# A two-network transformer trunk in fp32: first norm on its own loads, memory tokens normalized once, the keys' side of HGRN on GpSimd, rotary tables made during a network's first product

## The chip, the cores and the metric

The kernel runs on one core of a Trainium2 chip. A core has TensorE (PE, matrix products into PSUM banks), VectorE (DVE), ScalarE (ACT), GpSimd (POOL) and SyncE (SP, here only an issuer of DMAs). The metric is the device time of one execution, in microseconds (us). The kernel before has a median of 3372.84 us over 3 runs (3372.38 to 3385.61).

## The reference

The input is 256 tokens of width 1024, everything in float32. First come two layers of three mixers side by side, all fed by one norm and one wide projection; then a second trunk of two layers with SwiGLU networks, memory attention, and a convolution or a latent attention (MLA) as mixer.

```python
for l in range(2):                                   # the first trunk
    h = rmsnorm(x, norm_g[l]); proj = h @ w_in[l]    # width 1024 -> 19,712
    y_a = hgrn2_mixer(a_q, a_ff, a_fb, a_i, lbs[l])  # both directions, summed
    y_b = retention_mixer(b_q, b_k, b_v)             # rotary, both directions
    y_c = rwkv7_mixer(c_s)                           # delta rule, both directions
    x = x + (g0*(y_a @ w_a) + g1*(y_b @ w_b) + g2*(y_c @ w_c)) @ w_out[l]
x = rmsnorm(x, final_norm_g)
...
# second trunk, layer 0: network f00, convolution + memory, network f01
#               layer 1: shared keys and values from x, network f10, MLA queries + memory, network f11
def memory_attention(q_mem, mem, mem_norm_g, w_mem_kv, g_q, g_k):
    k, v = jnp.split(rms_norm(mem, mem_norm_g) @ w_mem_kv, 2, axis=-1)   # the same mem in both layers
    ...
def chunk_gla(q, k, v, log_f, strict):   # HGRN: o_t = q_t S_t, S_t = diag(f_t) S_(t-1) + k_t^T v_t
    decay = exp(b_i - b_j)               # b: cumulative sum of log f, per channel
    scores = sum(q_i * k_j * decay, axis=-1)
```

## The kernel before, in words

Each engine runs a program of its own, written in Python generators; semaphores (`then_inc`, `wait_ge`) tie them together. Weights come in chunks of up to 1 MB through a ring of five slots that SyncE fills in the order of use (`load_chunk`, L387). Every product is fp32; each matmul that the program writes is shown as two in the trace.

In the first trunk a layer's three mixers are woven together: R is RWKV, H is HGRN, B is retention. `weave` (L371) takes steps of three generators in the order of a string of the table `ORDER` (L144), one string for each engine; "R5 H2" means five steps of R and then two of H. So the order of the instructions on an engine is fixed by hand, and an engine that waits holds up all that stands behind it. Each mixer works in four quarters of two heads (RWKV: four) each.

**HGRN's levels** (`hgrn_dve` L1393, `hgrn_act` L1333, `hgrn_pe` L1280). The scores of a quarter are built in eight levels of block size, 128, 64, 32, ... 1. For each level VectorE makes the logarithms of the queries' and of the keys' decay (tiles `hg_qs` and `hg_ks`; L1454 to L1459 or L1474 to L1478), ScalarE takes Exp of both (L1373, L1374), VectorE multiplies them with the queries (L1481, 128x512) and the two halves of the keys (L1484, L1485, 128x256 each), TensorE multiplies keys and queries (L1311), and VectorE copies the block into the scores under a mask (L1494). Each level reuses the two tiles, so level n+1 begins when level n's product is done. GpSimd does only memsets and a few DMAs (`rwkv_pool`, L1015).

**A norm** (`norm_act` L456, `norm_dve` L478, `norm_pe` L440): per half of the tokens ScalarE sums squares (L463), VectorE makes the mean (L484), ScalarE the root (L467), VectorE the reciprocal (L487) and a diagonal matrix (L489), with which TensorE transposes and scales x (L450). VectorE and ScalarE copy the result with the gain to `h_features` (L497, L473). At the program's start VectorE and ScalarE wait for all three tables of constants (vectors, float constants, masks; L2945 to L2947) and make the lower bounds of HGRN before the first norm.

**The second trunk.** A SwiGLU network (`ffn_pe` L1836, `ffn_dve` L1994, `ffn_act` L1911) has 22 first products, one per weight chunk, with sums of operands made by VectorE two chunks ahead (`ffn_sums_dve`), and then 11 second products. Ahead of the convolution mixer and ahead of the queries the memory tokens are normalized: ScalarE squares them (L2213), takes the root (L2217), VectorE scales them into `mem_normed` (L2247). It is done once in each layer; since the tile `mem_tokens` is loaded twice (L2933, L2940), `mem_normed` also serves the networks as working space. Ahead of the shared keys VectorE makes the angles for the rotary tables (`rope_dve`, L2431, 17 small instructions with waits between) and ScalarE their Sines (`rope_act`, L2467).

## Time and profile before

| | us |
|---|---|
| median of 3 runs (lowest to highest) | 3372.84 (3372.38 to 3385.61) |
| the profiled execution's own time | 3378.15 |
| its span in the trace | 3376.3 |
| TensorE busy | 3126.1 (93%) |
| VectorE busy | 1762.8 (52%) |
| ScalarE busy | 709.1 (21%) |
| GpSimd busy | 61.5 (2%) |

The first trunk takes the first 2150 us or so (its first mixer layer 27 to 1082, its second up to 2147), the four networks 203 us each, and the rest are the mixers of the second trunk. Busy shares are means over these stages. A row of the timeline has its start, its length, the engine, the line of the kernel, what is written and read, and in square brackets how long the engine was idle before it and what released it.

### The profile page before, as it was taken

The numbers are of one execution on the slowest core, as the hardware profiler recorded it, in microseconds if no ns is written. First come the engines' busy times: TensorE is split into PE (matmuls) and PEld (weight loads), VectorE is DVE, ScalarE is ACT, GpSimd is POOL, SyncE is SP. The second block draws the span as 40 slices with busy tenths as digits, with TensorE's granted clock in tenths as the row PEclk, the third lists the DMA queues.
The fourth block names the chain that finished last, engine by engine and source line by source line (L and its number), as shares of the span: only waits on it lengthen the run. The fifth ranks groups of instructions, "written<-read, shape, count | busy, mean of one in ns | idle before, by whom it ended". The sixth has DMA issues, their size and how long they took to land.

```text
span 3376.3 us, 42896 instructions
## 1 busy us (share of the span) xinstructions
PE 3126.1 (93%) x17716; PEld 2610.1 (77%) x17716; DVE 1762.8 (52%) x3799; ACT 709.1 (21%) x1383; POOL 61.5 (2%) x70
## 2 busy tenths in 40 slices
PE   7999998999989999999899999899989979998999
PEld 6888887888876878788788887695849749855694
DVE  3555756374321474655646332475237647646475
ACT  2233323232111231332323110100111011013100
POOL 0000000000000000000000000000000000000000
PEclk9999998999989999999899999999989989997999
DMA  4323232324323422321331433444425423431343
GB/s 191 107 96 116 76 117 85 118 83 140 107 99 137 140 83 85 127 93 63 128 108 48 158 118 115 145 171 160 155 77 175 167 102 131 172 115 75 118 170 125
DMA packets 154018, 404.79 MB, mean 120 GB/s; under 512 B 57536, under 2 KB 106816, under 8 KB 109920
## 3 DMA queue, kind: packets, MB, share of 16 engines
q1 hardware_dynamic: 51376, 367.87, 30.4%
q10 hardware_dynamic: 100608, 28.32, 3.5%
q0 software_dynamic: 1840, 5.84, 0.5%
q8 instruction: 142, 2.33, 0.3%
q14 instruction: 52, 0.43, 0.0%
HBM read 389.41 MB, written 12.59 MB: 119 GB/s over the span
## 4 chain that ended last, share of the span: by engine, by line
PE 82%; DVE 10%; DMA 6%; issue 1%; ACT 1%; ACTq 0%; SPq 0%; DVEq 0%
PE bank L412 24%; PE bank L1865 16%; PE bank L1883 6%; PE bank L429 6%; PE bank L1689 5%; PE bank L1752 3%; PE bank L804 2%; DMA xT_scratch<-rw_bm 2%; PE bank L823 2%; PE bank L1311 2%; DMA rw_sig<-scores_scratch 1%; PE bank L1894 1%; DMA rw_ex<-xT_scratch 1%; DVE rw_ex L641 1%; PE bank L814 1%
## 5 line engine op out<-in xcount | busy, mean ns | idle before, releaser
L412 PE MATMUL bank<-h_features,weight_ring 128*128 128x256 f32 x4256 | 966.1, 383 | 7.4 <-DMA weight_ring<-in_w_in 2.9
L412 PEld LDWEIGHTS bank<-h_features,weight_ring 128*128 128x128 f32 x4256 | 802.1, 191 | 120.6 <-issue 5.7
L429 PE MATMUL bank<-weight_ring,h_features 128*128 128x256 f32 (+2 forms) x896 | 201.4, 376 | 2.6 <-DVE h_features L497 2.0
L429 PEld LDWEIGHTS bank<-weight_ring,h_features 128*128 128x128 f32 x896 | 161.5, 190 | 26.9 <-issue 4.0
L1865 PE MATMUL bank<-h_features,weight_ring 128*128 128x128 f32 x1408 | 171.9, 275 | 5.4 <-DVE h_features L497 5.4
L1865 PEld LDWEIGHTS bank<-h_features,weight_ring 128*128 128x128 f32 x1408 | 164.3, 192 | 6.1 <-DVE h_features L497 6.1
L1929 ACT COPY mem_normed<-bank 128x128 f32<-128x128 f32 x88 | 23.5, 267 | 485.9 <-PE bank L1865 474.6
L1689 PE MATMUL bank<-y_features,weight_ring 128*128 128x256 f32 x512 | 121.1, 384 | 0.0
L2006 DVE TENSOR_TENSOR mem_normed<-mem_normed,bank 128x256 f32<-128x256 f32 x88 | 37.1, 421 | 135.8 <-PE bank L1865 135.8
L1689 PEld LDWEIGHTS bank<-y_features,weight_ring 128*128 128x128 f32 x512 | 95.4, 191 | 12.8 <-issue 0.7
L450 PE MATMUL bank<-norm_diag,x_tokens 128*128 128x128 f32 x288 | 45.6, 330 | 58.8 <-DVE norm_diag L489 58.7
L804 PE MATMUL bank<-rw_bm,rw_scored_a 128*128 128x64 f32 x512 | 71.2, 285 | 27.1 <-DMA rw_ex<-xT_scratch 27.1
L1311 PE MATMUL bank<-hg_qs,hg_ks 128*128 128x128 f32 x512 | 76.0, 294 | 20.1 <-DVE hg_ks L1485 20.1
L450 PEld LDWEIGHTS bank<-norm_diag,x_tokens 128*128 128x128 f32 x288 | 43.6, 242 | 65.2 <-DVE norm_diag L489 44.9
L1865 PE MATMUL bank<-h_features,y_hgrn_features 128*128 128x128 f32 x704 | 93.0, 275 | 0.0
L1865 PE MATMUL bank<-y_rwkv_features,y_features 128*128 128x128 f32 x704 | 93.0, 275 | 0.0
L1865 PE MATMUL bank<-h_features,y_features 128*128 128x128 f32 x704 | 93.0, 275 | 0.0
L1865 PE MATMUL bank<-ff_silu,weight_ring 128*128 128x128 f32 x704 | 93.0, 275 | 0.0
L1865 PE MATMUL bank<-y_rwkv_features,y_hgrn_features 128*128 128x128 f32 x704 | 93.0, 275 | 0.0
L804 PEld LDWEIGHTS bank<-rw_bm,rw_scored_a 128*128 128x128 f32 x512 | 67.4, 202 | 30.5 <-issue 29.8
L1311 PEld LDWEIGHTS bank<-hg_qs,hg_ks 128*128 128x128 f32 x512 | 67.1, 202 | 28.7 <-DVE hg_ks L1485 19.8
L1865 PEld LDWEIGHTS bank<-y_rwkv_features,y_features 128*128 128x128 f32 x704 | 85.7, 192 | 0.0
(520 smaller groups left out, 5223.7 us busy)
## 6 DMA issues: line engine op xcount, KB each, us to landing
weight_ring<-in_w_in SPq DMA_DIRECT2D x146, 1024.0 KB, 4.9
weight_ring<-in_f00w SPq DMA_DIRECT2D x33, 1024.0 KB, 4.8
weight_ring<-in_f01w SPq DMA_DIRECT2D x33, 1024.0 KB, 4.8
weight_ring<-in_f10w SPq DMA_DIRECT2D x33, 1024.0 KB, 4.8
weight_ring<-in_f11w SPq DMA_DIRECT2D x33, 1024.0 KB, 4.8
weight_ring<-in_w_b SPq DMA_DIRECT2D x16, 1024.0 KB, 5.2
weight_ring<-in_w_out SPq DMA_DIRECT2D x16, 1024.0 KB, 4.9
weight_ring<-in_conv_in SPq DMA_DIRECT2D x10, 1024.0 KB, 4.9
```

Source lines behind the costliest of these rows:

```text
L412: m = e.matmul(bank[:, j, :], w[:, k, j * P:(j + 1) * P], x[:, k, :], start=k == 0, stop=k == kt - 1, skip_group_check=True)
L429: m = e.matmul(bank[:, t * n:(t + 1) * n], x[:, k, t * P:(t + 1) * P], w[:, k, :], start=k == 0, stop=k == kt - 1, skip_group_check=True)
L450: m = e.matmul(bank[:, k % 2, t * P:(t + 1) * P], x[:, t, k * P:(k + 1) * P], g.nm_diag[:, t, :], start=True, stop=True, skip_group_check= ...
L641: e.tensor_tensor(w[:, b], x.rearrange("p k t -> p t k").unsqueeze(1).to_broadcast(shape), y.unsqueeze(2).to_broadcast(shape), ALU.mult).t ...
L804: m = e.matmul(bank[:, h], R.scored_a[:, c, h, 0, :], src[:, h], start=True, stop=True, skip_group_check=True)
L823: m = e.matmul(bank[:, h], R.prod[:, h, :], dst[:, h], start=True, stop=True, skip_group_check=True)
L1311: m = e.matmul(bank[:, t, h, :], H.k_[:, h, t * P:(t + 1) * P], H.q_[:, h, i * P:(i + 1) * P], start=True, stop=True, skip_group_check=True)
L1689: m = e.matmul(bank[:, j, :], w[:, k, j * P:(j + 1) * P], y[:, c * KT + k, :], start=k == 0 and c == 0 and j == 0, stop=k == KT - 1 and c ...
L1752: m = e.matmul(banks[i], src[:, k0 + k, t * P:(t + 1) * P], w[:, k, s * 512:(s + 1) * 512], start=k0 + k == 0, stop=k0 + k == k_tiles - 1, ...
L1865: m = e.matmul(out, left[:, k, :], right[:, k, :], start=k == 0, stop=k == 3, skip_group_check=True)
L1883: m = e.matmul(banks[i], left, right, start=k == 0, stop=False, skip_group_check=True)
L2006: e.tensor_tensor(z[:, 0:2, :], z[:, 7:8, :].to_broadcast([P, 2, P]), first[:, 0:2, :], ALU.add).then_inc(*dve.up("u2", f, c))
```

## The change

1. **Start.** SyncE issues x, then the float constants, then the vectors, then the first weight chunk, and the masks behind it. The first norm waits for x and, at its diagonal, for the float constants; for the vectors only at the copy with the gain. The lower bounds come behind the norm. The operand of the dummy activation that loads the Sqrt table is a cell that GpSimd sets.
2. **Memory tokens.** They are normalized once, in place, during the first network (`memory_norm_act`, `memory_norm_dve`), and serve both layers; the second load goes.
3. **Keys' side of HGRN.** The four instructions per level on `hg_ks` move from VectorE to GpSimd (`hgrn_pool`), which is now woven from R and H. TensorE waits for both sides.
4. **Rotary tables.** The 17 small instructions become steps, one per chunk of the second network (f01); the Sines stand at its chunks 10 and 20.
5. The strings of `ORDER` for the mixers are rewritten on all engines, and those of `conv` and `queries` where steps have gone.

```diff
 ORDER = {
...
     ("mixers0", "vector"):
-        "H B R5 H2 R4 H2 R5 H R9 H9 R4 H6 R B H10 R H3 R4 H4 B R4 H3 R H11 R2 H4 R2 H R H2 B2 R2 H2 R2 H2 R5 H3 "
...
+        "H B R5 H2 R4 H2 R5 H R9 H12 R4 H R H2 B H5 R5 H3 B H5 R4 H2 R H8 R2 H2 R2 H2 R H B2 R4 H2 R B2 R4 B2 H3 "
...
+    ("mixers0", "gpsimd"):
+        "H R3 H13 R H7 R2 H12 R H12 R2 H4 R H12 R2 H4 R "
...
-def norm_act(e, g, key, x, x_ready, out, gain):
+def norm_act(e, g, key, x, x_ready, out, gain, first=False):
...
-    e.activation(g.nm_one, g.const("ones")[:, 0:1], ACT.Sqrt)
+    e.wait_ge(*g.st.pool.at("one"))
+    e.activation(g.nm_one, g.nm_one, ACT.Sqrt)
...
+    if first:
+        e.wait_ge(g.vectors_sem, 16)
...
-def norm_dve(e, g, key, out, gain, meanwhile=None):
+def norm_dve(e, g, key, out, gain, meanwhile=None, first=False):
...
+        if first and t == 0:
+            e.wait_ge(g.const_sem, 16)
         e.tensor_scalar(g.nm_diag[:, t, :], g.const("eye"), ss, None, ALU.mult).then_inc(*S.dve.up(key, "diag", t))
     if meanwhile:
         meanwhile()
+    if first:
+        e.wait_ge(g.vectors_sem, 16)
...
+            e.wait_ge(*S.pool.at("scale", l, q, level))
...
+            yield
+            e.wait_ge(*S.pool.at("logs", l, q, level))
             e.activation(H.k_, H.k_, ACT.Exp).then_inc(*act.up("expk", l, q, level))
...
-        bf4, bb4, q4, k4 = chunked(H.bf), chunked(H.bb), chunked(H.q_), chunked(H.k_)
+        bf4, bb4, q4 = chunked(H.bf), chunked(H.bb), chunked(H.q_)
...
-                e.tensor_copy(q4[:, :, 1, :], bf4[:, :, 1, :])
-                wf = H.totf.rearrange("p (n c) -> p n c", c=TT)[:, :, 0:1].to_broadcast([P, 2, P])
-                e.tensor_tensor(k4[:, :, 0, :], wf, bf4[:, :, 0, :], ALU.subtract)
-                wb = H.totb.rearrange("p (n c) -> p n c", c=TT)[:, :, 1:2].to_broadcast([P, 2, P])
-                e.tensor_tensor(k4[:, :, 1, :], wb, bb4[:, :, 1, :], ALU.subtract).then_inc(
-                    *dve.up("logs", l, q, level))
+                e.tensor_copy(q4[:, :, 1, :], bf4[:, :, 1, :]).then_inc(*dve.up("logs", l, q, level))
             else:
                 nb = 2 * T // (2 * level)
...
+                rf = level_first(H.bf, level)[:, :, level - 1:level].to_broadcast([P, nb, level])
+                rb = level_second(H.bb, level)[:, :, 0:1].to_broadcast([P, nb, level])
...
-                e.tensor_tensor(first(H.q_), first(H.bb), rb, ALU.subtract)
-                e.tensor_tensor(second(H.q_), second(H.bf), rf, ALU.subtract)
-                yield
-                e.tensor_tensor(first(H.k_), rf, first(H.bf), ALU.subtract)
-                e.tensor_tensor(second(H.k_), rb, second(H.bb), ALU.subtract).then_inc(*dve.up("logs", l, q, level))
+                e.tensor_tensor(level_first(H.q_, level), level_first(H.bb, level), rb, ALU.subtract)
+                e.tensor_tensor(level_second(H.q_, level), level_second(H.bf, level), rf, ALU.subtract).then_inc(
+                    *dve.up("logs", l, q, level))
...
-            e.tensor_tensor(H.q_, H.q_, H.q, ALU.mult).then_inc(*dve.up())
-            yield
-            e.wait_ge(*act.at("expk", l, q, level))
-            e.tensor_tensor(first(H.k_), first(H.k_), first(H.kf), ALU.mult).then_inc(*dve.up())
-            e.tensor_tensor(second(H.k_), second(H.k_), second(H.kb), ALU.mult).then_inc(
-                *dve.up("scale", l, q, level))
+            e.tensor_tensor(H.q_, H.q_, H.q, ALU.mult).then_inc(*dve.up("scale", l, q, level))
...
+def level_first(z, level):
+    if level == P:
+        return chunked(z)[:, :, 0, :]
+    return flat(z).rearrange("p (b s h) -> p b s h", s=2, h=level)[:, :, 0, :]
...
+def level_second(z, level):
+    if level == P:
+        return chunked(z)[:, :, 1, :]
+    return flat(z).rearrange("p (b s h) -> p b s h", s=2, h=level)[:, :, 1, :]
...
+def hgrn_pool(e, g, l):
...
+    for q in range(4):
+        for level in HG_SCALES:
+            yield
+            if level == P:
+                e.wait_ge(*pe.at("diag", l, q))
+                rf = H.totf.rearrange("p (n c) -> p n c", c=TT)[:, :, 0:1].to_broadcast([P, 2, P])
+                rb = H.totb.rearrange("p (n c) -> p n c", c=TT)[:, :, 1:2].to_broadcast([P, 2, P])
+            else:
+                nb = 2 * T // (2 * level)
+                e.wait_ge(*pe.at("scale", l, q, HG_SCALES[HG_SCALES.index(level) - 1]))
+                rf = level_first(H.bf, level)[:, :, level - 1:level].to_broadcast([P, nb, level])
+                rb = level_second(H.bb, level)[:, :, 0:1].to_broadcast([P, nb, level])
+            e.tensor_tensor(level_first(H.k_, level), rf, level_first(H.bf, level), ALU.subtract).then_inc(*pool.up())
+            e.tensor_tensor(level_second(H.k_, level), rb, level_second(H.bb, level), ALU.subtract).then_inc(
+                *pool.up("logs", l, q, level))
+            yield
+            e.wait_ge(*act.at("expk", l, q, level))
+            e.tensor_tensor(level_first(H.k_, level), level_first(H.k_, level), level_first(H.kf, level), ALU.mult
+                            ).then_inc(*pool.up())
+            e.tensor_tensor(level_second(H.k_, level), level_second(H.k_, level), level_second(H.kb, level), ALU.mult
+                            ).then_inc(*pool.up("scale", l, q, level))
+    yield
...
 def ffn_act(e, g, f, gain, x_ready):
...
+    if f == "f00":
+        memory_norm_act(e, g)
+    rope = rope_act(e, g) if f == "f01" else iter(())
     for at, c in enumerate(FFN_ORDER):
         ffn_first_act(e, g, f, at)
+        if at in (10, 20):
+            next(rope, None)
...
+    memory = memory_norm_dve(e, g) if f == "f00" else iter(())
+    rope = rope_dve(e, g) if f == "f01" else iter(())
+    next(memory, None)
     drain(ffn_sums_dve(e, g, f, 1))
     for at, c in enumerate(FFN_ORDER):
+        if at > 1:
+            next(memory, None)
+        next(rope, None)
...
 def memory_pe(e, g, l):
...
-    yield from to_features_pe(e, g, S, M.normed, KT, S.dve.at("normed", l), l)
+    yield from to_features_pe(e, g, S, M.tokens, KT, S.dve.at("normed"), l)
...
+def memory_norm_act(e, g):
+    S, M = g.me, g.M
+    e.wait_ge(g.mem_sem, 16)
+    for t in range(TT):
+        e.activation(g.nm_sq, M.tokens[:, t, :], ACT.Square, accum_out=M.ss[:, t:t + 1]).then_inc(*S.act.up("sum"))
+        e.wait_ge(*S.act.now())
+    e.wait_ge(*S.dve.at("mean"))
+    e.activation(M.ss, M.ss, ACT.Sqrt).then_inc(*S.act.up("root"))
...
+def memory_norm_dve(e, g):
+    S, M = g.me, g.M
+    e.wait_ge(*S.act.at("sum"))
+    e.tensor_scalar(M.ss, M.ss, 1.0 / D, EPS, ALU.mult, ALU.add).then_inc(*S.dve.up("mean"))
+    yield
+    e.wait_ge(*S.act.at("root"))
+    e.reciprocal(M.ss, M.ss).then_inc(*S.dve.up())
+    e.wait_ge(*S.dve.now())
+    for t in range(TT):
+        e.tensor_scalar(M.tokens[:, t, :], M.tokens[:, t, :], M.ss[:, t:t + 1], None, ALU.mult).then_inc(
+            *S.dve.up("normed"))
+        yield
...
 def memory_act(e, g, l):
...
-    e.wait_ge(g.mem_sem, 16 * (l + 1))
-    e.wait_ge(*g.rs.dve.at(f"f{l}0w2", 3))
+    e.wait_ge(*S.pe.at("w_mem", l, 0))
...
-    for t in range(TT):
-        a = e.activation(M.normed[:, t, :], M.tokens[:, t, :], ACT.Square, accum_out=M.ss[:, t:t + 1])
-    a.then_inc(*S.act.up("sum", l))
...
-    e.wait_ge(*S.pe.at("w_mem", l, 0))
...
 def memory_dve(e, g, l):
...
-    yield
...
-    for t in range(TT):
-        e.tensor_scalar(M.normed[:, t, :], M.tokens[:, t, :], M.ss[:, t:t + 1], None, ALU.mult).then_inc(
-            *S.dve.up("normed", l))
...
+        yield
...
+        yield
...
     for i, out in enumerate((g.sin_t, g.cos_t)):
         e.wait_ge(*S.dve.at("angle", i))
         e.activation(out, g.rope_r, ACT.Sin).then_inc(*S.act.up("sin", i))
+        yield
...
-    e.wait_ge(g.const_sem, 48)
+    e.wait_ge(g.const_sem, 16)
...
 def vector_program(e, g):
-    e.wait_ge(g.const_sem, 48)
-    lower_bounds_dve(e, g)
     for l in range(DEPTH):
-        drain(norm_dve(e, g, f"norm{l}", g.hT3, f"norm_g{l}"))
+        drain(norm_dve(e, g, f"norm{l}", g.hT3, f"norm_g{l}", first=l == 0))
+        if l == 0:
+            e.wait_ge(g.masks_sem, 16)
+            lower_bounds_dve(e, g)
...
-    e.wait_ge(g.const_sem, 48)
-    lower_bounds_act(e, g)
     for l in range(DEPTH):
-        drain(norm_act(e, g, f"norm{l}", g.x3, residual_ready(g, f"w_out{l - 1}") if l else None, g.hT3, f"norm_g{l}"))
+        drain(norm_act(e, g, f"norm{l}", g.x3, residual_ready(g, f"w_out{l - 1}") if l else None, g.hT3, f"norm_g{l}",
+                       first=l == 0))
+        if l == 0:
+            lower_bounds_act(e, g)
...
 def gpsimd_program(e, g):
     clear_scratch_pool(e, g)
     for l in range(DEPTH):
-        rwkv_pool(e, g, l)
+        weave(g, f"mixers{l}", "gpsimd", {"R": rwkv_pool(e, g, l), "H": hgrn_pool(e, g, l)})
...
-    e.wait_ge(*g.me.dve.at("normed", 0))
-    e.dma_start(g.M.tokens, g.t["mem"].rearrange("(t p) d -> p t d", p=P)).then_inc(g.mem_sem, 16)
 def sync_program(e, g):
     e.dma_start(g.x3, g.t["x"].rearrange("(t p) d -> p t d", p=P)).then_inc(g.x_sem, 16)
-    e.dma_start(g.vec[:, :], g.t["vectors"]).then_inc(g.const_sem, 16)
     e.dma_start(g.cf[:, :], g.t["const_f"]).then_inc(g.const_sem, 16)
-    e.dma_start(g.cm[:, :], g.t["const_m"]).then_inc(g.const_sem, 16)
+    e.dma_start(g.vec[:, :], g.t["vectors"]).then_inc(g.vectors_sem, 16)
+    w_in_load(e, g, 0, "codes")
+    e.dma_start(g.cm[:, :], g.t["const_m"]).then_inc(g.masks_sem, 16)
     for l in range(DEPTH):
-        w_in_load(e, g, l, "codes")
+        if l:
+            w_in_load(e, g, l, "codes")
...
```

On SyncE, at the program's start, before (`in_w_in` are the weight chunks, the first of them the codes'):

```order
L2944 DMA x_tokens<-in_x 128x2x1024
L2945 DMA vectors<-in_vectors 128x477
L2946 DMA float_constants<-in_const_f 128x1952
L2947 DMA mask_constants<-in_const_m 128x1408
L390 DMA weight_ring<-in_w_in 128x2048 x5
```

and in the changed kernel:

```order
L3001 DMA x_tokens<-in_x 128x2x1024
L3002 DMA float_constants<-in_const_f 128x1952
L3003 DMA vectors<-in_vectors 128x477
L394 DMA weight_ring<-in_w_in 128x2048
L3005 DMA mask_constants<-in_const_m 128x1408
L394 DMA weight_ring<-in_w_in 128x2048 x4
```

The vectors have moved behind the float constants, and the masks behind the first weight chunk.

On VectorE, in the first quarter of the first mixer layer, the first two levels of HGRN before:

```order
L1454 COPY hg_qs<-hg_bb 128x2x128
L1455 COPY hg_qs<-hg_bf 128x2x128
L1457 TENSOR_TENSOR hg_ks<-hg_totf,hg_bf 128x2x128
L1459 TENSOR_TENSOR hg_ks<-hg_totb,hg_bb 128x2x128
L1140 COPY_PREDICATED rw_bm<-mask_constants,bank 128x16x16
L1145 COPY_PREDICATED rw_ex<-mask_constants,bank 128x16x16
L1481 TENSOR_TENSOR hg_qs<-hg_qs,hg_q 128x512
L1484 TENSOR_TENSOR hg_ks<-hg_ks,hg_kf 128x2x128
L1485 TENSOR_TENSOR hg_ks<-hg_ks,hg_kb 128x2x128
L1474 TENSOR_TENSOR hg_qs<-hg_bb 128x4x64
L1475 TENSOR_TENSOR hg_qs<-hg_bf 128x4x64
L1477 TENSOR_TENSOR hg_ks<-hg_bf 128x4x64
```

and in the changed kernel on VectorE, and then on GpSimd:

```order
L1465 COPY hg_qs<-hg_bb 128x2x128
L1466 COPY hg_qs<-hg_bf 128x2x128
L1479 TENSOR_TENSOR hg_qs<-hg_qs,hg_q 128x512
L1153 COPY_PREDICATED rw_bm<-mask_constants,bank 128x16x16
L1158 COPY_PREDICATED rw_ex<-mask_constants,bank 128x16x16
L1474 TENSOR_TENSOR hg_qs<-hg_bb 128x4x64
L1475 TENSOR_TENSOR hg_qs<-hg_bf 128x4x64
```

```order
L1539 TENSOR_TENSOR hg_ks<-hg_totf,hg_bf 128x2x128 [waits hgrn_matmuls]
L1540 TENSOR_TENSOR hg_ks<-hg_totb,hg_bb 128x2x128
L1544 TENSOR_TENSOR hg_ks<-hg_ks,hg_kf 128x2x128 [waits hgrn_scalar]
L1546 TENSOR_TENSOR hg_ks<-hg_ks,hg_kb 128x2x128
L1539 TENSOR_TENSOR hg_ks<-hg_bf 128x4x64 [waits hgrn_matmuls]
L1540 TENSOR_TENSOR hg_ks<-hg_bb 128x4x64
```

All that writes `hg_ks` within the levels has left VectorE's row, and the queries' product has moved ahead of two masked copies of RWKV.

On TensorE, at the join from the third network (L1894, `ffn_pe`) to the norm of the queries, before:

```order
L1894 MATMUL bank<-y_hgrn_features,ff_act 128x512
L1894 MATMUL bank<-y_features,ff_act 128x512
L450 MATMUL bank<-norm_diag,x_tokens 128x128 x8
L2154 MATMUL bank<-float_constants,mem_normed 128x128 x4
L450 MATMUL bank<-norm_diag,x_tokens 128x128 x8
L429 MATMUL bank<-weight_ring,h_features 128x256 x16
```

and in the changed kernel:

```order
L1927 MATMUL bank<-y_hgrn_features,ff_act 128x512
L1927 MATMUL bank<-y_features,ff_act 128x512
L2198 MATMUL bank<-float_constants,mem_tokens 128x128 x4
L454 MATMUL bank<-norm_diag,x_tokens 128x128 x16
L433 MATMUL bank<-weight_ring,h_features 128x256 x16
```

The first four transposes of the memory tokens have moved from between the norm's halves to ahead of both.

## Rows read from the trace of the kernel before

**Rows 1.** The head of the page.

```profile
span 3376.3 us, 42896 instructions
```

**Rows 2.** Stretches: length, each engine's busy us (count), clock, DMA share, GB/s.

```profile
27.00:1082.00 1055.00, 990.11 (x5420) 851.23 (x5421) 520.70 (x1108) 273.29 (x475) 27.30 (x28) 0.96 0.32 108
...
2157.00:2360.00 203.00, 203.00 (x1385) 166.54 (x1385) 135.11 (x295) 17.54 (x50) 0.00 (x0) 1.00 0.46 161
```

**Rows 3.** TensorE's waits over the whole run, waited for: us, times, longest.

```profile
PE bank L804 <- DMA rw_ex<-xT_scratch: 27.1, 9, 6.1
PE bank L1311 <- DVE hg_ks L1485: 20.1, 10, 4.7
...
PE bank L788 <- DVE rw_scored_k L1114: 15.0, 6, 5.5
```

**Rows 4.** Timeline of the start: start, length, engine, line, [idle before, releaser].

```profile
1.73 0.42 SPq L2946 DMA_DIRECT2D float_constants<-in_const_f  x1
...
13.19 0.18 DVE L511 TENSOR_TENSOR small<-vectors 128x16 f32<-128x16 f32 x1 [13.19 <-DMA mask_constants<-in_const_m]
...
16.72 1.04 ACT L463 ACTIVATE y_rwkv_features<-x_tokens 128x1024 f32<-128x1024 f32 x1
...
20.33 5.75 PE L450 MATMUL bank<-norm_diag,x_tokens 128*128 128x128 f32 x32 [20.33 <-DVE norm_diag L489]
...
27.06 38.23 PE L412 MATMUL bank<-h_features,weight_ring 128*128 128x256 f32 x176 [0.98 <-ACT h_features L473]
```

**Rows 5.** DMA issues of the first 30 us, median us from issue to landing.

```profile
x_tokens<-in_x SPq DMA_DIRECT2D x1, 1024.0 KB, 5.0
float_constants<-in_const_f SPq DMA_DIRECT2D x1, 976.0 KB, 8.5
```

**Rows 6.** The weight ring in the first 30 us: loads and their landing.

```profile
L390 SPq DMA_DIRECT2D weight_ring<-in_w_in x5: 441/477/583, 2.9 to 4.9; - x5
...
DMA to landing us min/median/max: 13.2/18.1/21.8
```

**Rows 7.** Timeline at the join from the second SwiGLU network to the shared keys.

```profile
2728.92 0.68 DVE L2039 SCALAR_TENSOR_TENSOR x_tokens<-bank,x_tokens 128x512 f32<-128x512 f32 x1
...
2735.43 1.04 ACT L463 ACTIVATE y_rwkv_features<-x_tokens 128x1024 f32<-128x1024 f32 x1
...
2736.59 0.15 DVE L484 TENSOR_SCALAR norm_sum<-norm_sum 128x1 f32<-128x1 f32 x1 [2.88 <-ACT y_rwkv_features L463]
...
2737.55 5.67 PE L450 MATMUL bank<-norm_diag,x_tokens 128*128 128x128 f32 x32 [8.89 <-DVE norm_diag L489]
```

**Rows 8.** Timeline at the join from the first network to the convolution mixer.

```profile
2361.58 0.14 DVE L484 TENSOR_SCALAR norm_sum<-norm_sum 128x1 f32<-128x1 f32 x1
...
2364.61 5.70 PE L450 MATMUL bank<-norm_diag,x_tokens 128*128 128x128 f32 x32 [3.88 <-DVE norm_diag L489]
```

**Rows 9.** Timeline at the join from the third network to the queries.

```profile
3003.35 0.14 DVE L484 TENSOR_SCALAR norm_sum<-norm_sum 128x1 f32<-128x1 f32 x1
...
3006.36 2.64 PE L450 MATMUL bank<-norm_diag,x_tokens 128*128 128x128 f32 x16 [3.87 <-DVE norm_diag L489]
```

**Rows 10.** Line 1477 over the whole run: ns min/median/max, first and last start.

```profile
L1477 DVE TENSOR_TENSOR hg_ks<-hg_bf x56: 406/419/423, 132.7 to 1852.8; 128x256 f32<-128x256 f32 x56
```

**Rows 11.** Timeline of one level, the keys' Exp.

```profile
133.98 0.62 ACT L1374 ACTIVATE hg_ks<-hg_ks 128x512 f32<-128x512 f32 x1
```

**Rows 12.** GpSimd's timeline over the run.

```profile
16.39 0.33 POOL L1026 MEMSET rw_state<- 128x256 f32 x1
16.64 1.82 POOL L1031 MEMSET rw_scored_a<- 128x2048 f32 x1
...
647.34 1.93 POOL L1031 MEMSET rw_scored_a<- 128x2048 f32 x1 [125.13 <-PE bank L867]
```

**Rows 13.** VectorE's timeline, us 225 to 245 and then 646.5 to 651.

```profile
233.85 0.43 DVE L1416 TENSOR_SCALAR hg_bf<-hg_bf 128x512 f32<-128x512 f32 x1
...
647.55 1.99 DVE L1416 TENSOR_SCALAR hg_bb<-hg_bb 128x512 f32<-128x512 f32 x1
```

51 lines of the change are left out of this document (22 added, 29 removed), and 90 rows, old and new, of the table ORDER.

## The prediction

> **What bounds the kernel now.** I read the head and the busy shares first, then the table by stretches, then TensorE's waits, and last the timelines of the places that the change touches. The span is 3376.3 us [rows 1]. The stretches show TensorE as the bound nearly everywhere: in the first mixer layer it works 990.11 of 1055 us, in the first SwiGLU network 203.00 of 203 [rows 2]. So a layer has 65 us of idle TensorE to win, and a network none (the second layer is like the first). VectorE is busy 520.70 of the layer's 1055 us and 135.11 of the network's 203. TensorE's waits say where the idle time sits: 27.1 us, over the two layers, for the DMAs that bring the inverses back, which the change does not touch; 20.1 us in 10 waits for `hg_ks`, the keys' side of HGRN; 15.0 us for a mask that VectorE applies [rows 3]. The rest of the waits are the joins between stages, where one norm stands between two products; there everything is a serial chain, and removed work is removed time. The change works on both kinds.
>
> **The start (saved: 10.3 us).** Today VectorE and ScalarE wait until all three constant tables are in: the first instruction starts at 13.19, released by the masks, and then come the lower bounds with a table load; the first Square starts at 16.72, the norm's products at 20.33, the first projection at 27.06 [rows 4]. New: x first, then the float constants, and the norm waits for no more. x is issued two instructions of 0.5 us before the constants' 1.73, at 0.7, and lands 5.0 later, at 5.7 [rows 4, 5]. From a Square to the norm's first product it takes 2737.55 - 2735.43 = 2.1 us at the keys' join, where nothing disturbs [rows 7], so the chain is ready at about 8; the float constants decide. They land at 1.73 + 8.5 = 10.2 today [rows 4, 5]; without the small vectors table before them I take 9.6. Plus the diagonal and a hand-over, 0.35 to 0.4: products from 10.0 instead of 20.33. From there to the first projection I keep 27.06 - 20.33 = 6.7 us: projection from 16.7 instead of 27.06. Is its weight chunk there? Today the first of five lands 13.2 us after its issue at 2.9, at 16.1, with the masks (704 KB) ahead of it [rows 6]; now it goes ahead of the masks, so before 16. The masks then end near 16.1, and the lower bounds follow behind the norm, before the codes' product ends, 7 us after 16.7; nobody asks for them earlier. After that TensorE takes one chunk per 38.23 / 176 x 32 = 7 us, far slower than the loads come (the five are in by 26.7), so the lead is not eaten by them. Bounds: 9 us if the constants are no earlier than 10.2 and the hand-overs cost more, 11 if they land with x.
>
> **The rotary tables (saved: 7.0 us).** At the keys' join the last residual ends at 2728.92 + 0.68 = 2729.6; then VectorE makes the tables, and ScalarE's Sines and table loads hold the norm's Square back to 2735.43. The norm's mean runs at 2736.59 and the products start 0.96 later, at 2737.55 [rows 7]. Without the tables ScalarE's Square runs under the residual, as it does at the other joins, and the mean follows the residual at once, as at the conv join, where it starts at 2361.58, in front of the last residual's end. So products at 2729.6 + 0.96 = 2730.5: 7.0 us earlier. The seventeen tiny VectorE instructions and two Sines now stand in the second network, whose VectorE has (203 - 135.11) / 22 = 3 us to spare per chunk [rows 2]; one lands in each. A Sine with its table loads delays a silu by some 3 us twice, and TensorE's operands are made two chunks ahead: cost 0. Were that cover gone, the 4 us of tables and 5 us of table loads would come back there.
>
> **The memory tokens (saved: 4.1 us, two joins).** The mean runs at 2361.58, but the products start at 2364.61, not 0.96 after it, since two Squares of the memory tokens stand before the norm's root on ScalarE [rows 8]: 2.07 us. The same in the queries: 3003.35 to 3006.36, 2.05 us [rows 9]. The Squares are now done once, in the first network, beside its first chunk (2 x 1.04 us of ScalarE, as in rows 7, which works 17.54 of the network's 203; on VectorE two of about 0.8 us, by the 0.43 of half the width in rows 13, with the 3 us of room above); the second 1 MB load of the tokens goes. At the queries the first transposes of the tokens, which stood between the norm's halves on TensorE, now stand ahead of them, in its idle time; up to 1 us more may be won there, and I count none. Bounds 3 to 6.
>
> **Keys' side on GpSimd (saved: 6 us, bounds: 40 saved to 44 lost).** Per level VectorE loses four 128x256 instructions, `L1477`, `L1478`, `L1484`, `L1485`, of 0.419 us each [rows 10]; back to back they start every 0.33 us. 64 levels make 256 instructions and 85 us of VectorE. GpSimd gets 256. The trace has none of this kind; the nearest rows are its memset of the same shape, 0.33 us [rows 12], which reads nothing, and three times that, 1.0, for two streams in and one out. I take 0.7, between them. The path from one level's product to the next is today 3.5 us when VectorE is free: four subtractions, 3 x 0.33 + 0.42 = 1.4 us, two Exps of 0.62 that overlap a little, 1.2, two products, 0.76, and a hand-over [rows 10, 11]. New: 2 x 0.7, Exp 0.62, 2 x 0.7 and hand-overs of 0.2: 3.6. So the path is as long as it was, and what is won is VectorE's queue for others, where it is full. The longest wait for `hg_ks`, 4.7 us, is such a place [rows 3]. 85 us of the two layers' 2 x 520.70 us of VectorE is 8%. The layers' idle TensorE less the DMA waits is 130 - 27, about 100 us; I expect it to lose a tenth, 10 us, and to pay 4 of them back in the interference below: 6. The bounds: at best the 20.1 us for `hg_ks` and a quarter of the other 80 us; at worst the slow case below.
>
> The interference is real in this trace: the 128x512 tensor_scalar of `L1416` takes 0.43 us alone and 1.99 us when a GpSimd memset of 1.93 us runs (it takes 1.82 alone) [rows 12, 13]. VectorE stood still till GpSimd was through, and cost GpSimd 0.1 us. Whether tensor_tensor, which is most of VectorE's work here, is held as well, no row shows. The Trainium skill says so: "SBUF — State Buffer", section "SBUF: two separate sides", makes the port pair an exclusive lock, taken also by VectorE instructions with two SBUF inputs against a GpSimd instruction that reads SBUF. By that rule every one of the 256 can hold VectorE, also in the q side's step that starts at the same moment; the sum of this part would then be about 0 or a small loss instead of 6. And "GPSIMD Engine Reference", section "Elementwise — side-by-side cycle accounting", gives 2.6 cycles an element at 1.2 GHz, by which 256 elements take 0.56 us and some dispatch: that agrees with the value taken, and no row here shows it.
>
> The order tables are rewritten with it. In it a layer has 28 gaps between two levels of one quarter on TensorE. Counted with 38.23 / 176 = 0.217 us per matmul of 256 columns and two matmuls to each that the program writes [rows 4], six of the 28 hold 6 us of work or less, 4.7 in the mean, one of them under 2. A path of 3.6 fits in all but that one.
>
> **The sum.** 10.3 + 7.0 + 4.1 + 6 = 27.4 us. The profiled run's own time is 3378.15 for its span of 3376.3; less 27.4 it is 3350.8. The median of the runs is 5.3 us below that run, so I name 3345.
>
> **Rivals.**
> *More is won in the mixers.* The queue of VectorE gets short enough that the 20.1 us for `hg_ks` go almost entirely and the other mask waits by half; for it speaks that the longest of these waits is 1.2 us above the whole path, so that it is queue and not path; against it the interference. 3372.8 - 21.4 - 30 = 3321.
> *GpSimd only swaps one wait for another.* Its instructions take 1.0 us, and on the path two of VectorE's 0.42 get in between: 4 x 1.0 + 0.8 + 0.84 = 5.6 us. At both layers' 12 tight gaps (4.7) that is 11 us, and 5 more elsewhere, with the relief used up: 3372.8 - 21.4 + 16 = 3367. That is the case which the skill's lock rule makes more likely.
> *Slower: GpSimd becomes the bound of HGRN.* Place: the chain product, GpSimd subtraction, Exp, GpSimd product. At 1.5 us each the path is 4 x 1.5 + 0.8 = 6.8 us; at the 12 tight gaps (mean 4.7 us) 25 us are lost, and VectorE, held for 256 x 1.5 us and wanting to run half of that time, waits 190 us, a tenth of it on the path: 19. Net of 21.4: +22, 3395. It decides from about 1.4 us per instruction on. Against it: 1.4 is over four memsets.
> *The heads are hidden anyway.* The start's 10 us are taken back by the weight loads behind it, and the joins keep only half of theirs: 3372.8 - 5.6 - 6 = 3361. Against it speaks the loads' rate above.
>
> **How the numbers follow.** Half a per cent, 17 us, is about what a measurement of this kernel can tell from no change. Forecast (3333 to 3356): 0.46. More won: 0.18. Swap: 0.18. Slower: 0.13. Hidden: 0.05. Faster by over 17 us, below 3356: the first two, 0.64. Same: swap, hidden, and a little of the slower case, 0.23; slower 0.13. For 8 in 10 I leave out the upper half of the slower case and the tail below: 3313 to 3383. The forecast's own range is 3333 to 3356.
>
> **What would show it.** First projection at 16 to 18 us; products of the keys' norm about 1 us after the last residual, of the conv and queries norms 1 us after the mean; both networks still at 203 us with no idle TensorE. In the mixers: GpSimd's 128x256 tensor_tensor at 0.6 to 0.9 us, waits for `hg_ks` no larger than 20 us in sum, and 60 to 65 us of idle TensorE in a layer, as now. Wrong I would be with GpSimd over 1.2 us, with VectorE's tensor_tensor stretched from 0.42 to over 0.8 in most levels, or with idle TensorE over 75 us in a layer.

## The result and the profile after

The changed kernel takes 3361.12 us (median of 7 runs, 3354.36 to 3365.51), the kernel before 3377.34 us beside it (7 runs, 3372.38 to 3385.61). The ratio is 0.994, with a 95% interval of 0.9927 to 0.9953: 20 us faster, where 27.4 us were forecast (the two medians lie 16.2 us apart). The time named was 3345 us, with 3333 to 3356 as the forecast's own range: 3361.12 is above both, in part because the kernel before is at 3377.34 here, and the forecast started from 3372.84. The profiled execution is the slowest of the seven, 3365.51 us.

```profile
span 3363.7 us, 42903 instructions
```

Its stages against those of the profile before, in us. A stage runs from the first product of its norm to that of the next, as TensorE's timeline shows them; the last ends with the last matmul.

| | before | after | change | forecast |
|---|---|---|---|---|
| start, to the norm's first product | 20.3 | 10.1 | -10.2 | -10.3 |
| first mixer layer | 1058.5 | 1070.4 | +11.9 | -3 |
| second mixer layer | 1071.1 | 1070.7 | -0.4 | -3 |
| second trunk | 1221.0 | 1207.1 | -13.9 | -11.1 |

A second profile of the changed kernel gave 1071.4, 1065.2 and 1207.3 for the last three, so a layer's length is good to some 5 us. The first layer's loss is there both times, and without the new GpSimd work and strings that layer stays at 1061 us (`start_only` and `rest` below). In the second layer the idle time grew too, from 76 to 82.5 us; its length didn't, since the same matmuls are busy for 988 us in this profile and for 995 before. The timeline of the start (start, length, engine, line, in brackets the idle time before and what ended it), which answers to [rows 4]:

```profile
5.73 1.04 ACT L468 ACTIVATE y_rwkv_features<-x_tokens 128x1024 f32<-128x1024 f32 x1
...
9.67 0.29 DVE L498 TENSOR_SCALAR norm_diag<-float_constants,norm_sum 128x128 f32<-128x128 f32 x1 [2.18 <-DMA float_constants<-in_const_f]
...
17.40 14.91 PE L416 MATMUL bank<-h_features,weight_ring 128*128 128x256 f32 x68 [0.97 <-DVE h_features L508]
```

The constants decide, as said, and the first projection starts at 17.40, 9.7 us earlier. The joins, norm by norm, on TensorE and VectorE; they answer to [rows 7 to 9]:

```profile
2362.81 0.14 DVE L491 TENSOR_SCALAR norm_sum<-norm_sum 128x1 f32<-128x1 f32 x1
...
2363.76 3.84 PE L454 MATMUL bank<-norm_diag,x_tokens 128*128 128x128 f32 x32 [1.81 <-DVE norm_diag L498]
...
2726.47 0.68 DVE L2083 SCALAR_TENSOR_TENSOR x_tokens<-bank,x_tokens 128x512 f32<-128x512 f32 x1
2727.07 0.14 DVE L491 TENSOR_SCALAR norm_sum<-norm_sum 128x1 f32<-128x1 f32 x1
...
2728.03 2.16 PE L454 MATMUL bank<-norm_diag,x_tokens 128*128 128x128 f32 x17 [1.81 <-DVE norm_diag L498]
...
2991.18 0.14 DVE L491 TENSOR_SCALAR norm_sum<-norm_sum 128x1 f32<-128x1 f32 x1
...
2992.56 3.84 PE L454 MATMUL bank<-norm_diag,x_tokens 128*128 128x128 f32 x32 [1.79 <-DVE norm_diag L498]
```

The keys' norm starts 0.9 us after the last residual (2727.15), the convolution's 0.95 after the mean, the queries' 1.4. TensorE sits idle 1.8 us ahead of each, where it was 3.9 and 8.9. There is more in these rows than the waits: 32 matmuls of the convolution's norm take 3.84 us, and took 5.70 before [rows 8]. The stretch from the norm on, before and then after (length; busy us of PE, PEld, DVE, ACT, POOL; granted clock):

```profile
2364.00:2368.00 4.00, 3.32 (x19) 3.03 (x20) 2.55 (x9) 1.37 (x5) 0.71 (x1) 0.74 0.85 350
```

```profile
2363.00:2367.00 4.00, 3.24 (x29) 3.24 (x30) 1.76 (x7) 1.68 (x5) 0.06 (x1) 1.00 0.88 350
```

The granted clock was 0.74 after 3.9 us of idle TensorE, a mean over the levels 1.2 and 2.4 GHz, and 1.00 after 1.8 us.

The mixer layers tell the other half. The first one, and the first network, by stretches, answering to [rows 2]:

```profile
17.00:1084.00 1067.00, 990.10 (x5423) 848.88 (x5424) 501.37 (x993) 282.96 (x484) 127.34 (x158) 0.96 0.33 110
2158.00:2361.00 203.00, 202.95 (x1385) 166.63 (x1386) 136.62 (x299) 19.74 (x55) 0.00 (x0) 1.00 0.46 161
```

The network is full as before. The layer has 77 us of idle TensorE instead of 65. TensorE's waits over the whole run, answering to [rows 3] (waited for: us, times, longest):

```profile
PE bank L1325 <- DVE hg_qs L1479: 37.7, 6, 11.4
...
PE bank L799 <- DVE rw_scored_k L1127: 25.3, 7, 9.0
PE bank L815 <- DMA rw_ex<-xT_scratch: 19.9, 8, 4.5
...
PE bank L1310 <- DVE hg_ks L1457: 8.3, 3, 3.7
...
PE bank L1325 <- POOL hg_ks L1546: 3.0, 4, 0.9
```

The 20.1 us for `hg_ks` have become 3.0 for GpSimd and 37.7 for the queries' side, which never moved off VectorE. The 8.3 us at `L1310`, HGRN's product ahead of a quarter's levels, are new as well. GpSimd's new groups (busy us, mean ns; idle before), and then VectorE's queries' side, in which the same lines had means of 685, 423 and 419 ns before:

```profile
L1546 POOL TENSOR_TENSOR hg_ks<-hg_ks,hg_kb 128x256 f32<-128x256 f32 x64 | 60.9, 952 | 0.0
L1544 POOL TENSOR_TENSOR hg_ks<-hg_ks,hg_kf 128x256 f32<-128x256 f32 x64 | 54.5, 852 | 213.0 <-ACT hg_ks L1390 213.0
L1539 POOL TENSOR_TENSOR hg_ks<-hg_bf 128x256 f32<-128x256 f32 x56 | 37.7, 673 | 318.2 <-PE bank L1325 318.2
```

```profile
L1479 DVE TENSOR_TENSOR hg_qs<-hg_qs,hg_q 128x512 f32<-128x512 f32 x64 | 52.2, 816 | 15.3 <-ACT hg_qs L1387 15.2
...
L1474 DVE TENSOR_TENSOR hg_qs<-hg_bb 128x256 f32<-128x256 f32 x56 | 29.8, 531 | 11.9 <-PE bank L1325 8.6
...
L1475 DVE TENSOR_TENSOR hg_qs<-hg_bf 128x256 f32<-128x256 f32 x56 | 26.7, 476 | 0.0
```

All 256 of GpSimd's instructions take 201 us, 0.79 each in the mean, near the 0.7 taken. Over the two layers VectorE lost 107 us of instructions and got some 40 back in longer ones: of its summed times some 65 us are gone. One place, the level after which TensorE waits 6.3 us:

```profile
269.03 0.17 DVE L1207 TENSOR_SCALAR rt_mean<-rt_mean 128x4 f32<-128x4 f32 x1
269.06 0.72 POOL L1544 TENSOR_TENSOR hg_ks<-hg_ks,hg_kf 128x256 f32<-128x256 f32 x1 [1.74 <-ACT hg_ks L1390]
269.24 1.63 DVE L1209 TENSOR_TENSOR rt_o<-rt_o,rt_mean 128x1024 f32<-128x1024 f32 x1
269.75 1.70 POOL L1546 TENSOR_TENSOR hg_ks<-hg_ks,hg_kb 128x256 f32<-128x256 f32 x1
270.79 0.67 DVE L1215 TENSOR_REDUCE rw_var<-rw_kr 128x8 f32<-128x512 f32 x1
271.39 0.68 DVE L1479 TENSOR_TENSOR hg_qs<-hg_qs,hg_q 128x512 f32<-128x512 f32 x1
```

`L1209` takes 1.23 us alone and 1.63 here: it first waits for `L1544`, and then `L1546`, 0.72 alone, waits for it and takes 1.70. The two engines take turns. That is not what makes this wait, though: with all of HGRN on VectorE and the same strings it is 6.4 us (`dve_new` below). The other large wait, 11.4 us, has the order on VectorE and ScalarE in it:

```profile
557.31 3.33 DVE L1072 RECIPROCAL rw_sig<-rw_sig 128x512 f32<-128x512 f32 x1
...
561.29 0.42 DVE L1474 TENSOR_TENSOR hg_qs<-hg_bb 128x256 f32<-128x256 f32 x1
...
565.62 0.63 ACT L1387 ACTIVATE hg_qs<-hg_qs 128x512 f32<-128x512 f32 x1
...
566.53 1.86 DVE L1094 TENSOR_TENSOR_SCAN rw_bm<-float_constants,rw_sig 128x256 f32<-128x256 f32 x2
568.43 0.62 DVE L1097 COPY rw_tot<-rw_bm 128x4 f32<-128x4 f32 x1
568.96 0.68 DVE L1479 TENSOR_TENSOR hg_qs<-hg_qs,hg_q 128x512 f32<-128x512 f32 x1
```

The level's product was there at 556.7; the next level's subtraction stands behind RWKV's 3.3 us reciprocal and ends at 562.0. Its Exp on ScalarE starts only at 565.62, behind RWKV's sigmoids and two loads of activation tables. Its product then stands behind RWKV's scans and a tiny copy, held 0.62 us where it takes 0.17.

### The profile page after: what moved, and what is told of

Read it like the earlier page. It is cut to its first block, busy times and chain, and to the rows that moved or that the text cites. A ratio compares the mean times of both kernels' runs of the same rounds, so it can differ in the third digit from the quotient of the medians.

```text
span 3363.7 us, 42903 instructions
## 1 busy us (share of the span) xinstructions
PE 3119.5 (93%) x17716; PEld 2599.8 (77%) x17716; DVE 1713.8 (51%) x3539; ACT 723.0 (21%) x1389; POOL 256.2 (8%) x326
## 4 chain that ended last, share of the span: by engine, by line
PE 80%; DVE 12%; DMA 4%; ACT 2%; issue 1%; POOL 0%; ACTq 0%; DVEq 0%; SPq 0%
PE bank L416 23%; PE bank L1898 16%; PE bank L1916 6%; PE bank L1722 6%; PE bank L433 5%; PE bank L1785 3%; PE bank L815 2%; PE bank L834 2%; PE bank L1325 2%; DMA rw_ex<-xT_scratch 1%; PE bank L1927 1%; DVE rw_ex L652 1%; PE bank L825 1%; DMA xT_scratch<-rw_bm 1%; PE bank L454 1%
## 5 line engine op out<-in xcount | busy, mean ns | idle before, releaser
L416 PE MATMUL bank<-h_features,weight_ring 128*128 128x256 f32 x4256 | 981.6, 387 | 12.2 <-DVE y_features L1242 4.9
L1325 PE MATMUL bank<-hg_qs,hg_ks 128*128 128x128 f32 x512 | 76.4, 296 | 40.6 <-DVE hg_qs L1479 37.7
L1153 DVE COPY_PREDICATED rw_bm<-mask_constants,bank 128x256 f32<-128x256 uint32 x32 | 13.9, 436 | 154.6 <-PE bank L825 154.6
L1487 DVE COPY_PREDICATED hg_at<-mask_constants,bank 128x512 f32<-128x512 uint32 x56 | 41.0, 733 | 97.5 <-PE bank L1325 97.4
L1898 PEld LDWEIGHTS bank<-h_features,y_features 128*128 128x128 f32 x704 | 85.7, 192 | 0.0
```

The costliest lines, as they stand in the source:

```text
L416: m = e.matmul(bank[:, j, :], w[:, k, j * P:(j + 1) * P], x[:, k, :], start=k == 0, stop=k == kt - 1, skip_group_check=True)
L1325: m = e.matmul(bank[:, t, h, :], H.k_[:, h, t * P:(t + 1) * P], H.q_[:, h, i * P:(i + 1) * P], start=True, stop=True, skip_group_check=True)
L1487: e.copy_predicated(H.at.rearrange("p t h i -> p (t h) i"), mask, g.banks.get("scale", l, q, level).rearrange("p (n i) -> p n i", n=4)).th ...
L1898: m = e.matmul(out, left[:, k, :], right[:, k, :], start=k == 0, stop=k == 3, skip_group_check=True)
```

## The experiments

The ratios are to the kernel before, on the same chip; a thousandth is 3.4 us. "Idle" is TensorE's idle time in the two mixer layers of the profiled execution (before: 141 us, changed: 159).

| label | what it is | ratio | 95% interval | idle |
|---|---|---|---|---|
| start_only | before, with the new start | 0.9969 | 0.9959 to 0.9979 | 137 |
| rest | start, memory tokens, rotary tables | 0.9919 | 0.9898 to 0.9941 | 137 |
| pool_old | rest, and keys' side on GpSimd, old strings | 0.9966 | 0.9950 to 0.9982 | 144 |
| dve_new | rest, and new strings, keys' side on VectorE | 0.9973 | 0.9959 to 0.9988 | 165 |
| changed_again | all of the change | 0.9940 | 0.9926 to 0.9954 | 156 |
| side | rest, and useless work on GpSimd | 1.0039 | 1.0017 to 1.0060 | 167 |
| side_subs | rest, and half of that | 0.9970 | 0.9955 to 0.9985 | 154 |
| subs_pool | rest, and the keys' subtractions on GpSimd | 0.9916 | 0.9900 to 0.9932 | 137 |
| no_keys | rest without the keys' work | 0.9880 | 0.9860 to 0.9900 | 137 |
| order_fix | changed, three steps moved | 0.9935 | 0.9918 to 0.9951 | 158 |
| warm | rest, filled gaps | 0.9910 | 0.9891 to 0.9929 | 133 |
| warm_subs | subs_pool, filled gaps | 0.9904 | 0.9878 to 0.9930 | 135 |

**Which part gains, which loses.** `start_only` is the kernel before with the seven functions of the start taken from the change:

```diff
-    e.wait_ge(g.const_sem, 48)
-    lower_bounds_dve(e, g)
+        if l == 0:
+            e.wait_ge(g.masks_sem, 16)
+            lower_bounds_dve(e, g)
```

> The kernel before with the changed start alone. If the start's lead is kept: 10 us less, ratio 0.997, first projection at 17.4 us. If the weight loads or the first mixer layer take it back: 0.999 to 1.000, and the norm of the second layer starts at 1078 instead of 1068 us.

It measured 0.9969, 10.5 us: the start's lead is kept whole, and the first layer is as long as before in its profile (1061.2 us to 1058.5).

`rest` is the changed kernel with HGRN's functions and the mixers' strings of before (`rwkv_pool_all` runs `rwkv_pool` to its end):

```diff
-            e.wait_ge(*S.pool.at("scale", l, q, level))
...
-        weave(g, f"mixers{l}", "gpsimd", {"R": rwkv_pool(e, g, l), "H": hgrn_pool(e, g, l)})
+        rwkv_pool_all(e, g, l)
```

> The changed kernel with HGRN's functions and the mixers' order strings of the kernel before: start, memory tokens and rotary tables alone. The traces of before and after give 10.2 us for the start and 13.9 us for the second trunk, and 11.5 us lost in the mixers. Both theories (offload costs, strings cost) expect the mixers as long as before here: ratio 0.993 (24 us less), between 0.992 and 0.994. If instead the 11.5 us are the start's lead taken back in the first mixer layer, the ratio is 0.996.

0.9919: 27 us. The parts that are left gain more than the whole change does. The offload with its strings costs 7 us between the ratios, but their intervals overlap (0.9898 to 0.9941 and 0.9926 to 0.9954), so that these 7 us alone are not clear of zero. The 13 us between them and the 6 us of gain that were forecast are.

**GpSimd or strings.** `pool_old` keeps the offload and takes the old strings on four engines (two empty steps a level keep the counts); GpSimd's own string follows the times at which its steps ran before:

```diff
+        "R H R2 H12 R H4 R2 H16 R H12 R2 H4 R H14 R2 H2 R ",
-        "H R3 H13 R H7 R2 H12 R H12 R2 H4 R H12 R2 H4 R ",
```

> The changed kernel with the old order strings on TensorE, VectorE, ScalarE and SyncE; the keys' side stays on GpSimd, in the order in which its steps ran before. Theory A (the new strings cost the 11 us, the offload little): ratio 0.990 to 0.993, faster than the changed kernel. Theory B (the offload costs them, by a longer path and by VectorE's stretched instructions): 0.996 or more, and the waits for the keys' side on TensorE above 30 us.

0.9966, 16 us above rest: as theory B had it in time, but not by its sign in the trace, since TensorE's waits for the keys' side are 15.2 us, not above 30. With the 10.8 for the queries' side they are 26, where rest has 19.7 for `hg_ks`:

```profile
PE bank L1325 <- POOL hg_ks L1547: 15.2, 6, 4.5
...
PE bank L1325 <- DVE hg_qs L1479: 10.8, 4, 5.4
```

`dve_new` keeps the strings and puts the keys' instructions back on VectorE, behind the queries' ones:

```diff
             e.wait_ge(*act.at("expq", l, q, level))
-            e.tensor_tensor(H.q_, H.q_, H.q, ALU.mult).then_inc(*dve.up("scale", l, q, level))
+            e.tensor_tensor(H.q_, H.q_, H.q, ALU.mult).then_inc(*dve.up())
+            e.wait_ge(*act.at("expk", l, q, level))
+            e.tensor_tensor(level_first(H.k_, level), level_first(H.k_, level), level_first(H.kf, level), ALU.mult
+                            ).then_inc(*dve.up())
```

> The changed kernel with the new order strings, but the keys' four instructions per level on VectorE, right behind the queries' ones. Theory A (strings cost): as the changed kernel or slower, 0.994 to 1.000, with the 9.0 and 11.4 us waits still there. Theory B (offload costs): 0.991 to 0.993, and these waits fall below 6 us.

0.9973, 18 us above rest, with the waits of 9.0, 6.4 and 11.7 us in its trace, and no GpSimd work beside them: here theory A holds.

```profile
PE bank L1324 <- DVE hg_ks L1485: 40.6, 10, 11.7
PE bank L799 <- DVE rw_scored_k L1127: 26.8, 8, 9.0
```

The run isn't quite the strings by themselves, since the keys' instructions stand in the queries' steps, where the old strings had steps of their own for them. So neither theory alone holds. Each half costs 16 to 18 us by itself, both together 7: the strings suit the offload, and it wins back 11 us within them, but the pair doesn't reach the old strings with all on VectorE. `changed_again` is the changed kernel on one chip with others:

> The changed kernel itself beside the others on one chip: 0.994, between 0.993 and 0.995 as measured; the profile again with 9.0 and 11.4 us waits in each layer.

0.994 once more, with the same two waits in each layer.

**Interference by itself.** `side` is rest, with four tensor_tensor of GpSimd a level that nobody needs; they read constants and write `norm_diag`, and start when the offload's would. Each waits for the one before it, and takes 0.90 us in the mean, where the offload's take 0.79:

```diff
+            for i in range(2):
+                e.tensor_tensor(out, a, b, ALU.subtract).then_inc(*S.pool.up())
+                e.wait_ge(*S.pool.now())
+            yield
+            e.wait_ge(*S.act.at("expk", l, q, level))
```

> The kernel without the offload (label rest, ratio 0.9919), and beside it GpSimd runs four 128x256 tensor_tensor per level on tiles of its own (constants in, norm_diag out), released at the points where the offload's are; nobody waits for them within the layer. It adds work without use, so that interference stands alone. Theory I (VectorE's stretched instructions are what the offload costs): ratio 0.995 to 0.997, like pool_old. Theory P (the keys' path through GpSimd costs it): 0.991 to 0.993, although VectorE's instructions are stretched by 25 to 45 us in sum.

1.0039: 41 us above rest, more than either theory said, with no one waiting for GpSimd within the layer. Theory P's part that interference is harmless is out; that the path costs as well is not. VectorE's instructions under GpSimd's are 83 us longer than the same ones alone, and half of that reaches the end. TensorE's first wait, and three of VectorE's groups (418, 417 and 417 ns in rest):

```profile
PE bank L1349 <- DVE hg_ks L1523: 40.8, 25, 7.5
```

```profile
L1523 DVE TENSOR_TENSOR hg_ks<-hg_ks,hg_kb 128x256 f32<-128x256 f32 x64 | 41.9, 655 | 0.0
L1513 DVE TENSOR_TENSOR hg_qs<-hg_bf 128x256 f32<-128x256 f32 x56 | 41.4, 739 | 0.0
L1522 DVE TENSOR_TENSOR hg_ks<-hg_ks,hg_kf 128x256 f32<-128x256 f32 x64 | 36.8, 575 | 0.0
```

`side_subs` drops the two beside the products:

```diff
-            e.wait_ge(*S.act.at("expk", l, q, level))
-            for i in range(2):
-                e.tensor_tensor(out, a, b, ALU.mult).then_inc(*S.pool.up("side", l))
```

> As side, but GpSimd runs only the two instructions per level that start with the subtractions; the two beside the products are gone. It adds half of the useless work. Dose theory (each GpSimd instruction costs alike by what it holds up): half of side's loss, ratio 0.998 (0.996 to 1.000), VectorE stretched by about 40 us. Place theory (instructions that start when a product is done hit VectorE at the head of the level's chain, and cost most): above 1.000; or, if the ones beside the products cost most, 0.992 to 0.994.

0.997, 17 us above rest, with 37 us of longer instructions: the dose theory, near enough.

**What there was to win.** `subs_pool` is pool_old with the keys' products back on VectorE, so that GpSimd makes the subtractions alone:

```diff
-            e.tensor_tensor(level_first(H.k_, level), level_first(H.k_, level), level_first(H.kf, level), ALU.mult
-                            ).then_inc(*pool.up())
```

> pool_old with the two products of the keys back on VectorE: GpSimd makes only the two subtractions of each level. Theory P says that the products cost most, since they stand last in the path, at 0.73 to 1.7 us each, while the subtractions run beside the queries' ones: ratio 0.991 to 0.993, waits for hg_ks and hg_qs on TensorE below 20 us in sum. Theory I expects half of pool_old's loss: 0.994.

0.9916, as rest. The time is what theory P said; its reason, that the products cost most because they stand last, was not tested apart from their interference. VectorE's instructions are 18 us longer here, against 37 in side_subs, whose two take 0.86 us each where these take 0.67. At half of that some 9 us would be lost, and the 128 instructions fewer on VectorE would have to make up for it; the time fits, but no run separates the two.

`no_keys` leaves the keys' work out:

```diff
-            e.wait_ge(*S.pool.at("logs", l, q, level))
-            e.activation(H.k_, H.k_, ACT.Exp).then_inc(*act.up("expk", l, q, level))
+            e.activation(H.k_, H.kf, ACT.Exp).then_inc(*act.up("expk", l, q, level))
```

> pool_old without the four keys' instructions of each level on any engine: ScalarE takes Exp of the keys' gate in their place, so the scores are not the reference's. VectorE is relieved as in pool_old, nothing on GpSimd interferes, and the level's path is shorter by two subtractions and two products. That is an upper bound of what the offload could win. If the relief is real and the interference eats it: ratio 0.982 to 0.987, some 17 to 34 us below rest's 0.9919. If the relief is small in itself, because other waits take over: 0.988 to 0.992, and the idle time of TensorE in the two layers stays above 125 us (137 in rest).

0.988, 13 us below rest, the small case. The waits for the keys are gone, and others have come: 20.1 us for `rw_scored_k` and 11.9 for `rw_a`, 137 us of idle TensorE as before.

```profile
PE bank L799 <- DVE rw_scored_k L1127: 20.1, 4, 6.8
...
PE bank L766 <- DVE rw_a L1122: 11.9, 4, 5.7
```

So 13 us, good to about 10 by the intervals, is the most that taking the keys off VectorE could bring with the old strings, and pool_old, 29 us above no_keys, shows what doing them on GpSimd costs. VectorE's instructions are 35 us longer in pool_old; at side's rate of a half that is some 17 us. The other 12 of the 29 would be the keys' own path, with products of 0.87 and 0.89 us in the mean; no run separates it.

**The two long waits.** `order_fix` moves three steps of the changed strings in each layer, one excerpt on VectorE:

```diff
-        ... R B H2 R H B R2 H2 R H2 B
+        ... R B H3 R H B R2 H R H2 B
```

> The changed kernel with three steps moved in its order strings, in both layers. VectorE: the subtractions of one level ahead of RWKV's 3.3 us reciprocal, its queries' product right behind that reciprocal; in another level the queries' product ahead of retention's mean. ScalarE: both Exps of the first level ahead of RWKV's two sigmoids. If the strings put these behind too much: the waits of 11.4 and 6.3 us for hg_qs fall below 5 each, TensorE's idle time by 6 to 8 us a layer, ratio 0.990 to 0.992. Rival, the wait only moves to RWKV's own chain (L766, L799): ratio 0.993 to 0.995.

0.9935, from 0.994: nothing that can be told apart. The 11.4 us wait fell to 5.9, and 6.2 us came behind it at the next product of HGRN. The 6.3 us wait fell to 4.7, which is now one for GpSimd; those waits are 12.4 us in all and were 3.0:

```profile
PE bank L799 <- DVE rw_scored_k L1127: 30.9, 8, 9.0
...
PE bank L1325 <- DVE hg_qs L1479: 14.4, 4, 5.9
...
PE bank L1339 <- DVE hg_at L1487: 12.5, 2, 6.2
PE bank L1325 <- POOL hg_ks L1546: 12.4, 6, 4.7
```

The wait moved, as the rival had it, though mostly to HGRN and GpSimd; RWKV's chain got 5.6 us of it (`L799`, 30.9 for 25.3).

**The clock.** `warm` fills the two gaps of 7.1 and 8.1 us ahead of the norms of the first and third network:

```diff
+        if t == 0 and key in ("f00", "f10"):
...
+            for _ in range(14):
+                e.matmul(bank[:, 0, :], g.cf[:, 0:P], g.cf[:, P:P + T], start=True, stop=True, skip_group_check=True)
```

> The kernel without the offload (rest), with 14 matmuls of constants (128x256, results overwritten) ahead of the norms of the first and third network, where TensorE sits idle 7.1 and 8.1 us and then runs the norm's products at half its clock, in 5.6 to 6.3 us. If the idle time is what lowers the clock: products in 3.8 us at a granted clock of 1.00 there, 4 us in all, ratio 0.991. If the clock falls for another reason: still over 5.5 us, 0.992 or more.

0.991, 3 us below rest, within the noise, but the trace speaks. First rest, then warm, from the norm on:

```profile
2145.00:2149.00 4.00, 3.60 (x17) 3.60 (x18) 3.07 (x9) 1.07 (x3) 0.00 (x0) 0.50 0.00 0
```

```profile
2142.00:2145.00 3.00, 1.92 (x15) 1.52 (x14) 1.82 (x8) 2.11 (x6) 0.00 (x0) 1.00 0.00 0
2145.00:2149.00 4.00, 2.50 (x23) 2.31 (x21) 3.96 (x9) 2.31 (x5) 0.00 (x0) 1.00 0.00 0
```

The clock stayed at 1.00, and the norm's products took 3.84 us, not 6.30. At the second place it held in warm_subs (3.84 us) but not in warm (5.46, at a clock of 0.69), although the gaps left were 2.5 and 2.1 us: a short gap is not all that decides, and what else does stays open.

> subs_pool (only the keys' subtractions on GpSimd, old strings) with the same 14 matmuls. If both add up: ratio 0.990, about 4 us below subs_pool's 0.9916, and the best kernel of the study.

0.9904, the lowest of the full kernels, 32 us below the kernel before; its gain over subs_pool is within the intervals. The changed kernel is at 0.994. Between rest, subs_pool, warm and warm_subs the order is within the noise.

## Why the forecast came out as it did

The sum came out near, 27.4 us said and 20 measured, partly by luck: the joins gave some 6 us more than was said and the keys' side some 13 less, two errors with nothing to do with each other that half cancel.

**The start** was right: 10.3 us said, 10.2 in the trace up to the norm's first product (9.7 up to the first projection) and 10.5 by start_only. The bound was the constants, as read from [rows 4, 5], and the loads did not take the lead back.

**Rotary tables and memory tokens** were right in mechanism and too low in size: 11.1 us said, and 13.9 in the second trunk of the changed kernel, 16.2 in that of rest, 17 between the ratios of rest and start_only. The waits went as computed: from the norm of the second network to that of the keys it was 218.4 us and is 211.3, 7.1 less, against 7.0. What the sum lacked is the clock. It took the norms' products at their old length; three norms' products went from 5.3 to 5.7 us to 3.8, with 1.8 us of idle TensorE ahead of them and not 3.9 or 8.9; warm shows that filling such a gap has this effect. It was to be read in the trace before, where [rows 7 to 9] stand against the norm of the last network:

```profile
3161.40 3.84 PE L450 MATMUL bank<-norm_diag,x_tokens 128*128 128x128 f32 x32 [1.60 <-DVE norm_diag L489]
```

Part of the gain is given back in the queries' stage, 155.0 us before and 156.2 after, where the granted clock over the whole stage is 0.81 and was 0.83.

**The keys' side** is the step that failed. Its durations held: 0.79 us an instruction for 0.7, and TensorE waits 3.0 us for GpSimd's last product. Its net did not: 6 us saved were forecast, and by the ratios 7 were lost with the new strings and 16 with the old ones. The Trainium skill, "GPSIMD Engine Reference", section "Elementwise — side-by-side cycle accounting", had given an estimate of 0.56 us and some dispatch; alone they take 0.61 and 0.72. The relief, a tenth of the idle time or 10 us, was taken near the most there was to have (13 us, no_keys), since RWKV's masks and `rw_a` are late next. The mis-sized term is the interference: 4 us taken, while VectorE's instructions got 40 us longer and, by side and side_subs, nearly half of such time, here some 20 us, reaches the end. The forecast did not look at when they fall: GpSimd's subtractions start when the queries' do, at the head of each level, so the engines collide by design. The Trainium skill, "SBUF — State Buffer", section "SBUF: two separate sides", makes VectorE and GpSimd exclude each other: VectorE's instructions in a 2-port performance mode, and those with two SBUF inputs against a GpSimd one that reads SBUF. By that rule the forecast had "about 0 or a small loss", which was nearer than the value taken. It also fits what is held here and what isn't, with the copies and tensor_scalar under its first condition; that they run in such a mode no row shows. Of the 40 us, the instructions that the timeline shows singly make up some 35. In the changed kernel, under GpSimd's tensor_tensor, 85 executions of VectorE's tensor_tensor with two named SBUF sources took 15.7 us longer in sum, and 52 with one tile read twice 10.5; 26 copies and 8 tensor_scalar from SBUF took 9.0. With a source in PSUM, 49 masked copies took 0.2 us longer together, and 8 tensor_tensor, 4 tensor_scalar and 3 scalar_tensor_tensor nothing; nor did 10 reduces and 8 reciprocals.

**The strings** were not priced at all. The forecast counted the gaps between two levels on TensorE, which it found wide enough, and not what stands on VectorE ahead of the queries' product. dve_new shows 18 us for them without the offload, of which the offload wins back 11. One of the signs named for being wrong tripped: 77 us of idle TensorE in a layer, over the 75 set. The sign on the waits for `hg_ks`, 20 us, didn't see it, since TensorE now waits 37.7 us for the other tile, `hg_qs`, which no sign covered.

Of the rivals, "swaps one wait for another" came nearest in mechanism: 3.0 and 37.7 us for 20.1. But dve_new has the two large waits without GpSimd, so that in the changed kernel the strings did most of the swapping; pool_old, with 15.2 and 10.8 for 19.7, shows the rival's own. It put 16 us as lost in the mixers, from GpSimd instructions of 1.0 us on the path; measured are 7, with 0.79 us an instruction and VectorE's own made longer. "The heads are hidden anyway" named 3361 us, the time measured, and that is chance: start_only keeps the whole 10 us of the start, and the joins gave more than was said, not half.

## What to carry to other kernels

Work moved from VectorE to GpSimd is not free for VectorE: price the moved instructions at both engines wherever VectorE's neighbours are tensor_tensor, copies or tensor_scalar that read SBUF alone, and by these rows prefer what runs beside reads of PSUM, reduces or nothing. Before moving it, leave it out: a kernel without the work tells in one run the most that the move can win with the order as it is, here 13 us. And where a join gets shorter, look at the clock behind it, since a wait removed can bring its products down as well.

## What the runs showed of the hardware

- GpSimd's 128x256 float32 tensor_tensor takes 0.61 us alone for the levels' subtractions, in which one operand is broadcast, and 0.72 for their products. It is not the operation that makes the difference: side's subtractions of two plain operands take 0.72 too. It takes up to 1.70 when VectorE gets in first (1.80 in side).
- VectorE's 128x256 tensor_tensor takes 0.42 us alone and up to 0.96 behind one of GpSimd's; a copy of 4 columns 0.17 and 0.62. Instructions with a PSUM source are spared (49 masked copies, 0.2 us longer together).
- TensorE's products of a norm between two stages take 3.84 us at a granted clock of 1.00, behind 1.6 to 1.8 us of idle time. Behind 3.9 us they took 5.3 to 5.7, and behind 7 to 10 us 5.6 to 6.6; in rest and in the kernel before the clock was then 0.50 at their start and 0.59 to 0.67 over all of them.
- The same 17,716 matmuls are busy for 3109 us in the profile of dve_new and for 3134 in that of rest. That is the clock of the two profiled executions, 0.962 and 0.956: busy time times clock is 2991 and 2996 us. From run to run of one kernel the time follows the clock as well: of the kernel before, 25 runs beside these go from 3369.5 us at 0.958 to 3389.7 at 0.954. So differences of a few us between two profiles are read from idle time, and those between kernels from many runs.
- Idle time in a profile and the time of many runs do not go one for one: in the layers dve_new has 28 us more idle time than rest and is 18 us slower, pool_old has 7 more and is 16 us slower. More idle time did not bring a higher clock either: side has the most, 167 us, with a mean clock of 0.956 over its 12 runs, no_keys 137 with 0.960 over 5. Why the clock differs stays open.
